# Column-group modulation, four projection banks, two tiles of a top-k search counted by ScalarE, and the softmax division moved behind attention

## The reference: one step of a hybrid decoder layer

```python
mod = jax.nn.silu(c) @ w_ada + b_ada                    # 9 conditioning rows, 6 x 1024 columns
xn = rms_norm(x, norm1_g) * (1 + sc1) + sh1
qa, ka, va, qb, kb, vb, iq, ik, iw = split_proj(xn @ w_in)
...
# mixer B: for each query the top k = min(256, L//4) causal keys by the indexer's score
scores = jnp.where(causal[None], scores, -jnp.inf)
_, sel = lax.top_k(scores, topk)
...
# both mixers
p = jnp.exp(s - m)
l = jnp.sum(p, axis=-1, keepdims=True)
o = jnp.einsum('...qk,...kd->...qd', p / l, v)
...
x = x + g1 * (o @ w_out)
x = x + g2 * ((jax.nn.silu(gate) * up) @ w_down)
```

## Time and profile before

| | us |
|---|---|
| median of 3 runs | 1939.26 (1938.38 to 1940.05) |
| profiled execution | 1938.74 |
| its span in the trace | 1937.1 |
| PE busy, of the span | 1755.0 (91%) |
| DVE busy | 944.3 (49%) |
| ACT busy | 668.4 (35%) |
| POOL busy | 535.5 (28%) |

### The profile page before, as it was taken

One profiled execution on the slowest core, in us unless ns is written; L12 is line 12 of the kernel. 1 busy time (PEld: TensorE's weight loads), 2 busy tenths in 40 slices (PEclk: granted clock), 3 DMA queues, 4 the chain that ended last, 5 costly groups with the idle time before them and its releaser, 6 DMA issues. The chain is left out here.

```text
span 1937.1 us, 30827 instructions
## 1 busy us (share of the span) xinstructions
PE 1755.0 (91%) x11234; PEld 1607.0 (83%) x11234; DVE 944.3 (49%) x2225; ACT 668.4 (35%) x1784; POOL 535.5 (28%) x661
## 2 busy tenths in 40 slices
PE   6697778989984999999878989999999999999998
PEld 4495367877873788888848979999999999999998
DVE  2705697887894677777643162232133033123124
ACT  4415423321321888888713233111111111211111
POOL 0334234541453222121012205223222222321310
PEclk8898799999996999999988999999999999999999
DMA  7600013344214112110055012112111111111002
GB/s 232 231 23 13 5 42 113 105 132 138 78 56 133 65 55 88 33 62 1 5 200 198 23 44 69 57 28 64 44 32 54 43 43 43 43 43 43 22 1 90
DMA packets 137907, 135.37 MB, mean 70 GB/s; under 512 B 7085, under 2 KB 126813, under 8 KB 137158
## 3 DMA queue, kind: packets, MB, share of 16 engines
q1 hardware_dynamic: 136150, 131.07, 21.3%
q0 software_dynamic: 1648, 2.89, 0.5%
HBM read 115.29 MB, written 27.04 MB: 73 GB/s over the span
## 5 line engine op out<-in xcount | busy, mean ns | idle before, releaser
L2424 DVE TENSOR_TENSOR hf<-bank,sg 128x352 f32<-128x352 f32 x66 | 34.6, 525 | 464.9 <-PE bank L2172 455.3
L2172 PE MATMUL bank<-ahi,gwh 128*128 128x352 f32 x1056 | 196.2, 327 | 11.3 <-DVE hf L2424 6.7
L2333 POOL TENSOR_TENSOR hlo<-hf,hhi 128x352 fp32r<-128x352 f32 x66 | 62.7, 949 | 505.1 <-ACT hhi L2262 505.1
L2437 DVE SCALAR_TENSOR_TENSOR x<-wide,modT,x 128x352 f32<-128x352 f32 (+1 forms) x264 | 151.3, 573 | 96.8 <-PE wide L2188 96.8
L2172 PE MATMUL bank<-alo,gwh 128*128 128x352 f32 x1056 | 192.6, 324 | 2.0 <-DVE alo L2413 2.0
L2172 PE MATMUL bank<-ahi,gwl 128*128 128x352 f32 x1056 | 194.2, 326 | 0.0
L2172 PEld LDWEIGHTS bank<-ahi,gwh 128*128 128x128 f32 x1056 | 176.2, 190 | 14.0 <-DVE hf L2424 7.0
L1164 DVE TENSOR_SCALAR_CACHE_REDUCE junk<-sig,cand 128x896 uint8<-128x896 f32 (+6 forms) x217 | 177.8, 878 | 0.6
L2172 PEld LDWEIGHTS bank<-alo,gwh 128*128 128x128 f32 x1056 | 174.9, 189 | 2.7 <-DVE alo L2413 2.7
L2172 PEld LDWEIGHTS bank<-ahi,gwl 128*128 128x128 f32 x1056 | 176.5, 191 | 0.0
L1526 PE MATMUL bank<-diag,prob 128*128 128x128 f32 x1152 | 167.1, 282 | 5.4 <-ACT diag L1662 4.7
(11 more groups left out here) (298 smaller groups left out, 3443.6 us busy)
## 6 DMA issues: line engine op xcount, KB each, us to landing
raw<-in_w_ada SPq DMA_DIRECT2D x24, 1024.0 KB, 5.4
gw<-in_w_gate_up SPq DMA_DIRECT2D x44, 512.0 KB, 5.1
raw<-in_w_in SPq DMA_DIRECT2D x11, 1024.0 KB, 5.7
dw<-in_w_down SPq DMA_DIRECT2D x22, 512.0 KB, 3.6
scr_x<-xT SPq DMA_DIRECT2D x1, 4224.0 KB, 16.2
xnat<-in_x_prompt SPq DMA_DIRECT2D x8, 512.0 KB, 5.6
scr_q<-ubuf SPq DMA_DIRECT2D x32, 128.0 KB
qn<-scr_q SPq DMA_DIRECT2D x8, 512.0 KB, 3.9
```

The lines of the kernel that those rows point to most:

```text
L2172: mm = pe.matmul(pb[2 * s + side][:, 0:THIRD], a[r][:, k, side, :], b[:, k, third(th)], start=(p == 0 and k == 0), stop=(p == 2 and k == K ...
L2333: pool.tensor_tensor(hlo[:, r, third(th)], hf[:, (3 * r + th) % 2, :], hhi[:, r, third(th)].bitcast(F32), ALU.subtract).then_inc(h_lo, 1)
L2424: v.tensor_tensor(hf[:, s, :], pb[2 * s + 1][:, 0:THIRD], sg[:, s, :], ALU.mult).then_inc(h_mul, 1)
L2437: ins = v.scalar_tensor_tensor(out=x1[:, d, cols], in0=src[:, 0:n], scalar=modT[:, 40 + d, 0:1], in1=x1[:, d, cols], op0=ALU.mult, op1=ALU ...
```

## The change

1. *Modulation chunks.* The conditioning columns `cT` are padded from 9 to 32, and the eight matmuls of a chunk go to four groups of 32 columns of the array, two to each group. The whole 128 × 256 bank is copied, and the turn becomes a matmul with a 0/1 matrix `modsel` (128 × 9) that adds the four groups. Late chunks alternate between two pairs of banks. Their turns come after the first units of the next projection, and the bias add moves from DVE to ACT in the late chunks and stays on DVE in the first eight.
2. *Units* of the late stage use four banks (two of them halves of a wide bank) instead of two.
3. *Search.* ACT counts tiles 4 and 5 (896 and 1024 keys) with Sign and a sum (`tally_wide`); their threshold is kept negated, and the comparison is with 2k − width. DVE counts the other five. Since a tie gives Sign 0, two exact counts on DVE (`next_up`) after the last bit settle ties. A bit is now two steps, not three.
4. *Attention.* `diag`, its reciprocals and its scalings are gone: the turn of `prob` is a plain transpose, row sums are kept.
5. *Sample attention* begins with one reciprocal of all row sums; POOL widens them in 16 copies (`rexp`), PE turns them (`spread_inverse`), and DVE multiplies the attention output by them (`scale_rows`), interleaved with the loop over sequences.
6. Several pairs of semaphores are merged into one.

The diff, cut to its core:

```diff
 def ada(n):
-    if a >= 1:
+    if a >= ada_at + 2:
+        pe.wait_ge(ada_nat, a - 1)
+    elif a >= 1:
         pe.wait_ge(ada_nat, a)
     for k in range(KD):
-        mm = pe.matmul(ada_bank[a][0][0:9, 0:WCH], cT[:, k, :], raw[:, n % 3, k, :],
-                       start=(k == 0), stop=(k == KD - 1))
+        j = 32 * (k % 4)
+        mm = pe.matmul(ada_bank[a][0][j:j + 32, 0:WCH], cT[:, k, :], raw[:, n % 3, k, :],
+                       start=(k < 4), stop=(k >= 4))
 def ada_turn(a):
...
-        mm = pe.transpose(ada_bank[a][1][:, j * 9:j * 9 + 9], modn[:, a % 2, j * P:(j + 1) * P],
-                          ident[0:9, 0:9])
+        mm = pe.matmul(ada_bank[a][1][:, j * 9:j * 9 + 9], modn[:, a % 2, j * P:(j + 1) * P],
+                       modsel[:], start=True, stop=True)
 def project(n, turns=()):
...
-        if u >= 2:
+        if u >= NIDX + 4:
+            pe.wait_ge(unit_read, u - 3)
...
-        dst = bank[u % 2][:, 0:w]
+        dst = unit_bank(u)[:, 0:w]
...
+        if t < len(turns):
+            ada_turn(turns[t])
# ACT
+def tally_wide(q):
+    act.wait_ge(cand_ready, q + 1)
+    for a in (4, 5):
+        last = act.activation(tally[...], sig[:, ioff[a]:ioff[a] + width[a]], ACT.Sign,
+                              bias=cand[:, a:a + 1].bitcast(F32), accum_out=cnt[:, a:a + 1])
+    last.then_inc(wide_tally, 1)
...
     unit(u)
     root(u - 1)
+    if turns:
+        ada_bias(turns.pop(0))
+    for q in tallies_after.get(u - NIDX, ()):
+        tally_wide(q)
# DVE
 def decide(b):
+    v.wait_ge(wide_tally, BITS - b)
     joined()
-    link(v.tensor_tensor(nok[:], cnt[:], kp[:], ALU.is_lt))
+    link(v.tensor_tensor(nok[:], cnt[:], kc[:], ALU.is_lt))
...
+        v.tensor_scalar(cand[:], cand[:], 1 << (b - 1), None, ALU.bitwise_xor).then_inc(cand_ready, 1)
+        v.wait_ge(cand_ready, BITS + 1 - b)
...
-    steps += [lambda b=b: count(b, 0), lambda b=b: count(b, 1), lambda b=b: decide(b)]
+    steps += [count, lambda b=b: decide(b)]
+steps += [next_up, thresholds]
# attention
-    mm = pe.matmul(dst[...], prob[:, a % RING, j * P:(j + 1) * P], diag[:, a % 4, :],
-                   start=True, stop=True)
+    mm = pe.transpose(dst[...], prob[:, a % RING, j * P:(j + 1) * P], ident[:])
...
-    pe.wait_ge(diag_in, a + 1)
+    pe.wait_ge(s_exp, a + 1)
...
-    act.activation(diag[:, m % 4, :], ident[:], ACT.Copy, scale=rinv[:, m % 4:m % 4 + 1]).then_inc(diag_in, 1)
...
-    v.reciprocal(rinv[:, m:m + 1], rowsum[:, m:m + 1]).then_inc(r_sum, 1)
# sample attention, POOL, ahead of the vpg loads
+    for u in range(16):
+        p, g = divmod(u, 2)
+        if u >= 4:
+            pool.wait_ge(spread, u - 3)
+        pool.tensor_copy(rexp[:, u % 4], rinv[...].to_broadcast([P, 4, 2, HD])).then_inc(widened, 1)
# PE, after each half of the turned keys
+    def spread_inverse(u):
+        pe.wait_ge(widened, u + 1)
+        if u == 0:
+            pe.wait_ge(qe, 1)
+        else:
+            pe.wait_ge(scaled, u)
+        for j in range(4):
+            mm = pe.transpose(bank[0][:, j * P:(j + 1) * P], rexp[:, u % 4, j]..., ident[:])
+        mm.then_inc(spread, 1)
# DVE, between kTa and kTb, and after kTb
+    def scale_rows(u):
+        v.wait_ge(spread, u + 1)
+        v.tensor_tensor(oT[:, p, 512 * g:512 * g + 512], oT[...], bank[0][:], ALU.mult).then_inc(scaled, 1)
```

More of the change, by code:

```diff
@@ L257, in front, with slot_of @@
     assert T.end <= LB + 18432 + 8192
+    tally = T.at("tally", [P, 896 + 1024], BF16, LB + 18432 + 4352)
+    assert T.end <= LB + 18432 + 8192
+    joff = ioff[0:4] + [ioff[4] + NEWW, 0, ioff[4]]
+    BITS = 31
+    NSLOT = 9 * (NTILE + 1) - 5
+    NSTEPS = 2 + 2 * BITS + 2 + 7
+    def slot_of(step):
+        return next(s for s in range(NSLOT) if -(-NSTEPS * (s + 1) // NSLOT) > step)
+    tallies_after = {}
+    for q in range(BITS):
+        tallies_after.setdefault(slot_of(1 + 2 * q) + 1, []).append(q)
     n_pool = A["cache_idx_k"].shape[1]
@@ L279, in front, with unit_bank @@
     NIDX = 3 * (NTILE + 1)
-    ada_bank = [(bank[0], bank[1]) if a < ada_at else (bank[2], bank[3]) for a in range(len(adas))]
+    ada_bank = [(bank[0], bank[1]) if a < ada_at else (bank[2 + a % 2], wide[1][:, 512 * (a % 2):512 * (a % 2) + 512])
+                for a in range(len(adas))]
+    late_bank = [bank[0], bank[1], wide[0][:, 0:512], wide[0][:, 512:1024]]
+    def unit_bank(u):
+        return bank[u % 2] if u < NIDX else late_bank[(u - NIDX) % 4]
     START = (["x0", "x1", "x2", "small", "x3", "x4", "ada0", "x5", "x6", "ada1", "x7", "x8", "ada2", "rs", "ada3"]
@@ L691, in _ @@
             indexer()
-            turn = None
+            turns = []
             for n in range(ada_at + 3, len(order)):
                 if n in ada_no:
-                    if turn is None:
+                    if ada_no[n] == ada_at:
                         pe.wait_ge(ix_acc, 49)
                     ada(n)
-                    turn = ada_no[n]
-                    ada_turn(turn)
-                else:
-                    project(n)
+                    turns.append(ada_no[n])
+                else:
+                    project(n, turns)
+                    turns = []
+            for a in turns:
+                ada_turn(a)
         @block.scalar
@@ L719, in ada_evac, with ada_bias @@
                     act.wait_ge(ada_tr, a - 1)
-                act.activation(modn[:, a % 2, :], ada_bank[a][0][0:9, 0:WCH], ACT.Copy).then_inc(ada_nat, 1)
+                act.activation(modn[:, a % 2, :], ada_bank[a][0][:, 0:WCH], ACT.Copy).then_inc(ada_nat, 1)
+            def ada_bias(a):
+                act.wait_ge(ada_tr, a + 1)
+                for j in range(2):
+                    last = act.activation(modT[:, 2 * a + j, :], ada_bank[a][1][:, 9 * j:9 * j + 9], ACT.Identity,
+                                          bias=vecT[:, 2 * a + j:2 * a + j + 1])
+                last.then_inc(ada_done, 1)
             def split_w(n):
@@ L841, in _ @@
                         copy_out(7 + 2 * h)
+            def tally_wide(q):
+                act.wait_ge(cand_ready, q + 1)
+                for a in (4, 5):
+                    last = act.activation(tally[:, ioff[a] - ioff[4]:ioff[a] - ioff[4] + width[a]], sig[:, ioff[a]:ioff[a] + width[a]], ACT.Sign,
+                                          bias=cand[:, a:a + 1].bitcast(F32), accum_out=cnt[:, a:a + 1])
+                last.then_inc(wide_tally, 1)
             pj = [n for n in range(ada_at + 3, len(order)) if n not in ada_no]
@@ L862, in _ @@
             root(len(units) - 1)
+            for a in turns:
+                ada_bias(a)
         @block.gpsimd
@@ L1144, in orient @@
                 link(v.tensor_tensor(kp[:], kp[:], tk[:, 2, :], ALU.add))
+                joined()
+                link(v.tensor_scalar(kc[:], kp[:], 1.0, None, ALU.mult))
+                joined()
+                for a in (4, 5):
+                    link(v.tensor_scalar(kc[:, a:a + 1], kp[:, a:a + 1], 2.0, float(-width[a]), ALU.mult, ALU.add))
                 for a, r, o, w in tiles():
@@ L1265, in attention @@
     nmax = T.at("nmax", [P, 4], F32, T.end)
-    rowsum = T.at("rowsum", [P, 4], F32, T.end)
-    diag = T.at("diag", [P, 4, P], F32, T.end)
-    rinv = T.at("rinv", [P, 4], F32, T.end)
     KT = PAST // P
@@ L1766, in sample_attention @@
     rsum = T.at("rsum_s", [P, 4], F32, T.end)
+    rexp = T.at("rexp", [P, 4, 4, 2, HD], F32, T.end)
     n_pool = A["cache_k"].shape[1]
     assert T.end <= S["loaded"]
+    rowsum, rinv = S["rowsum"], S["rinv"]
     ldc = sem("s_consts")
+    inv = sem("s_row_inverse")
+    spread = sem("s_inverse_spread")
+    scaled = sem("s_rows_scaled")
+    widened = sem("s_inverse_widened")
     k_in = [sem(f"s_k_in{r}") for r in range(3)]
@@ L1875, in _ @@
                 mm.then_inc(sc, 1)
+            pe.wait_ge(scaled, 16)
             for x in range(4):
```

154 lines of the change are left out of this document (94 added, 60 removed).

## The result

The changed kernel takes 1854.34 us (median of 4 runs, 1852.26 to 1858.17) against 1938.82 of the kernel before in the same comparison: a ratio of 0.9567, interval 0.9550 to 0.9584. That is 84 us faster, where 137 were forecast, and 4 us beyond the upper end of the range. The profiled execution took 1854.12 us, its span is 1852.0.

What follows compares the result with a forecast made beforehand. PE was taken as the busiest engine in each stage, so the change was worth what it took off PE's chain. 1938.7 − 87 (late) − 58 (attention) + 17.5 (sample attention) − 9 (start) = 1802 us; forecast 1785 to 1820, range 1770 to 1850.

Steps and rivals of the forecast that it cites:

- Late projections, −87 forecast: Late projections: 276 us instead of 363, from 256 of PE's work plus 5, 12 and 3; bounds −70 and −100.
- the one on banks: Late projections: four banks give ACT about 8.6 us before PE stops; 17.7 us of stalls gone except in the first projection.
- 12 us for handovers: Late projections: allowance for handovers between DVE and ACT and the selections at the end, 12 us.
- prices of the chunks, the passes and the tallies: Late projections: a chunk about 1.0 us, DVE's dropped passes 71 us in all, ACT's pairs of Sign 71 us in all.
- Attention, −58 forecast: Attention: 289 us instead of 347, as PE loses 66 us of work; ends −66 and −42.
- busy share of 90%: Attention: PE's 258 us divided by 0.90 give 287 us; the −42 end assumed PE 84% busy.
- Rival 2: Attention: held by ACT and DVE, PE only waits for banks; −25 in place of −58, total 1835 us, chance 0.12.
- Sample attention, +17.5 forecast: Sample attention: page loads behind POOL's copies end near 1020 us and the values wait for them; +11 to +24.
- Start, −9 forecast: Start: five chunks at 1.0 us would save 13, but weight loads and DVE's normalization limit it; −5 to −12.
- Rival 1: Late search: DVE's decisions wait in series for ACT's tallies, 7.6 us a round against 6.2; 43 us, total 1845, chance 0.15.
- Rival 4: Attention: turns drop the clock from 2.4 to 1.2 GHz; PE's 258 us become up to 460, total 1993, chance 0.05.
- little but turns: Sample attention, 978 to 998 us: PE does little but turns at a granted clock of 1.00, cited against the clock falling.

Runs made afterwards that it cites:

- six buffers: The changed kernel with six instead of four buffers for units on their way out and the squares' scratch in bf16: 1838.69 us, ratio 0.9487.
- POOL's copies: The changed kernel with POOL instead of ACT making the high halves of the next head's queries and keys in attention: 1838.25 us, ratio 0.9482.
- the shorter remainder: The changed kernel with DVE computing the probabilities' remainder in attention for only 32 of each 128 queries: 1842.81 us, ratio 0.9506.
- the pages between: The changed kernel with POOL issuing the 16 page loads of sample attention between its copies instead of behind all of them: 1849.72 us, ratio 0.9543.
- the search on DVE alone: The changed kernel with all seven tiles counted on DVE again, without ACT's tallies or the tie count: 1876.25 us, ratio 0.9667.

## Why the prediction was wrong, step by step

The 52 us by which the forecast was too low are 28 in the late stage, 18 in attention, 4 in sample attention and 2 in the gap between the first two.

*Late projections, −87 forecast, −59 measured.* The step that failed is the one on banks: stalls that "I count [...] as gone except in the first projection", with 12 us for handovers. PE idles for 34 us in place of the forecast's 20, and behind its stops some of its matmuls run at the lower clock (270 us busy, 261 with six buffers). The prices of the chunks, the passes and the tallies were close. What I left out is a unit's way out of the bank: evacuation, the root behind the next evacuation, DVE's scaling between counts, POOL's gains behind a weight split, the store, and a ring of four buffers over it all. Before the change the 11.4 us of a pair of chunks let that way catch up, and I took those pauses away without asking what had used them. ACT's waits for stores stood in the trace of before too, 63 us, and I left them out, because ACT was "not the bound". These are ACT's waits of before, 242 to 605 us:

```profile
ACT ubuf L754 <- PE bank L587: 146.4, 55, 11.0
...
ACT ubuf L754 <- DMA scr_q<-ubuf: 24.2, 8, 7.7
ACT ubuf L754 <- DMA out_v_p<-ubuf: 20.3, 3, 9.4
...
ACT ubuf L754 <- DMA out_win_k_p<-ubuf: 12.4, 4, 5.4
...
ACT ubuf L754 <- DMA out_win_v_p<-ubuf: 6.0, 1, 6.0
```

The waits for stores grew by only 11 us with the change, but ACT's waits for PE's units fell from 146 to 43 us: ACT had lost the slack behind which the stores were hidden. That the pauses were this slack is my reading; no run gave six buffers to the kernel before, so what they are worth there is open. With six buffers PE's late stage is 276.3 us, the 276 of the forecast, but this agreement is in part luck: the gap is then 26.4 us, and stage and gap together are 303 where the forecast left 290 (276 and the 14 of before). The stop at the second chunk of the first pair, 10.3 us, was to be read in the changed code and isn't in my sum.

*Attention, −58 forecast, −40 measured.* The work removed was right to the microsecond (258.7 of PE for 258). The step that failed is dividing it by a busy share of 90% for the stage: PE is busy 84%, the lower end that I had given. A share over a stage hides that in a head of mixer A ACT holds three steps and PE five; only the latter could gain what PE lost. Rival 2 had the right kind of cause, another engine's pace, but for the whole stage, and its −25 was too little; its sign came, 32 us of waiting for `pL`. ACT's relief was mis-sized as well: 50.6 us were taken off it, and its busy time fell by 37 (284.0 to 247.1), because the rows of the scalings overlap their neighbours, as was allowed for in DVE's passes but not here. POOL's copies give 13 of the missing 18 us back; what DVE's remainder costs is shown only by the shorter remainder, 9 us, and these two were not run together.

*Sample attention, +17.5 forecast, +22 measured.* The mechanism was right, the page loads behind the copies: the values started at 915.44, waiting 5.1 us for `vpg`. The mis-sized term is what follows, taken as unchanged: from the values' start to the end of the stage it takes 15.8 us, 12.7 before. The first run of 16 value matmuls takes 3.64 us as against 3.27 in the earlier trace rows, and after the wait the clock stays low for longer: the granted clock is 0.50, the lower level, from 915.44 to 924.40, and the second such run takes 3.64 us as well (1.92 with the pages between).

*Start, −9 forecast, −9 measured; back 0 forecast, −1 measured.* Right. The gap ahead of attention grew by 2 us, which wasn't in the sum.

*Rival 1* (the search locks to ACT): its sign came, just, as DVE's decisions wait 30.1 us for tallies. But the search on DVE alone costs 22 us, and with six buffers these waits are still 25.6 us while PE's late stage is 276.3; so they aren't what held PE, and the rival's 43 us didn't come. *Rival 4* (the clock falls in attention) didn't come: the granted clock of that stage is 0.97, as before. On this the Trainium skill, "TensorE: Matmul & The Clock Gate", Part 4: PE-mode transpose, says that transposes don't bring the full clock; a stage with 576 turns among its matmuls doesn't show it. The stretch that the prediction set against this rival was less pure than "little but turns" says: beside 73 turns it holds 80 matmuls of scores. And the rival's price was low, since 258 us are up to 516 at half the clock, not 460.

*Left open:* why the gap ahead of attention is 26 us with six buffers. In the trace DVE's selections stand in the way of the last scalings up to 514.4, and behind them ACT waits for stores again (8 us), but no run moved either alone. Open too is what holds PE in attention once POOL makes the copies, beyond the waits for `pL`.

## What to carry to other kernels

When a change takes pauses away from the busiest engine, list what used those pauses: the buffers of the results on their way out, and the preparation of the next operands. Count the links and buffers of that way against the new pace, in the trace of before, even where the engine on it is idle most of the time, since its idle time may be a wait for a buffer. And take the bound from each step of a loop, not from the busy shares of the stage.

## What the runs showed of the hardware

A scaling of 128 x 256 on DVE that takes 0.42 us when it is alone took 3.33 us while POOL split weights. The rows of DVE in the changed kernel; POOL's split ran from 334.95 to 339.47:

```profile
332.52 0.42 DVE L1311 TENSOR_TENSOR ubuf<-ubuf,rs 128x256 f32<-128x256 f32 x1
...
336.42 3.33 DVE L1311 TENSOR_TENSOR ubuf<-ubuf,rs 128x256 f32<-128x256 f32 x1
339.68 0.17 DVE L1308 RECIPROCAL rs<-sd 128x4 f32<-128x4 f32 x1
```

DVE's operation ended just behind POOL's. The Trainium skill, "GPSIMD Engine Reference", 1. Specifications, says that POOL shares its SBUF interfaces with VectorE, with contention for VectorE's instructions that run in a 2-port mode or have two SBUF inputs; this scaling has two, and the row agrees. DVE's counts, with one tensor input, kept their 0.5 to 1.0 us throughout, under a split too. But one tensor input doesn't save every operation: the one that writes a selection's mask took 4.6 us under the split from 493.50 to 498.44, where the same operation on 128 x 640 took 0.49 us without a split.

```profile
L1288 DVE TENSOR_SCALAR mask_b<-sig 128x512 bf16<-128x512 f32 x1 | 4.6, 4605 | 0.0
```

No row tells in which mode it ran. This isn't new with the change: in the kernel before, the six scalings that fell into a split took 3.3 to 3.4 us. A Sign over 1024 keys with its sum took 1.169 us, a tenth more than the Square over 1024 columns of the earlier trace rows, and one over 896 keys 1.069 us.
